# A third branch's up units for tokens 128 to 255 moved behind the first expert query, on a one-core hybrid decoder layer

## The chip, the core and the metric

One core of one Trainium2 chip runs the whole layer in one launch. The metric is the device time of an execution in microseconds (us), lower is better. Engines are named as the profile names them: PE is TensorE, with PEld its weight loads, DVE is VectorE, ACT is ScalarE, POOL is GpSimd, SP is SyncE; SPq, ACTq and POOLq are their DMA queues.

## The reference, cut to what matters

256 tokens of width 1024, all in float32. Three branches (sparse attention, RWKV-7 time mixing, cross-attention into 256 memory tokens) each give 512 values per token. They are projected up, gated and summed, projected out, and added to x. A PEER layer follows: 8 heads choose 16 of 16,384 experts per token, and each expert is one row of `u` (dotted with the token) and one row of `v` (added with the weight).

```python
up = jnp.einsum('bscw,cwd->bscd', branches, w_up.astype(F32))
gates = jax.nn.sigmoid(gate_p.reshape(B, S, N_BRANCH, D).astype(F32) + gate_bias.astype(F32))
merged = jnp.sum(gates * up, axis=2).astype(h.dtype)
h = h + merged @ w_out
h = h + peer_ffn(rmsnorm(h, ffn_norm_gain), peer_w_q, peer_key1, peer_key2, peer_u, peer_v)
...
# in peer_ffn: q = xn @ w_q; scores against two key tables; top 16 of each side; top 16 of the 256 sums
hid = jax.nn.gelu(jnp.einsum('td,ted->te', xt.astype(F32), ue), approximate=False)
return jnp.einsum('te,ted->td', gt * hid, ve).astype(xt.dtype)
```

## The kernel before

**Two tiles of tokens.** Tile 0 is tokens 0 to 127, tile 1 is tokens 128 to 255. Nearly all of on-chip memory is one tensor, `pool_mem`, cut by hand into parts that are used again as their earlier contents are done.

**The first part.** Projections, attention, memory attention and RWKV run in an order written out by hand, `SCHEDULE`. Weights come as blocks of 1 MB (`BLOCK`, 2048 columns) through a ring of three (`wring`), which SP refills when the projection unit that used a block is done (`proj_full`). Products go to two PSUM banks in turns (`begin_unit`, `begin_bank`, `unit_read`).

**The up units.** There are 12, four to a branch, two to a weight block. Branch order is memory, attention, RWKV. Units 8 to 11 (RWKV) need `y_rwkv`, which comes from `ytok` after the group norm, by PE transposes (job `("yt", t)`) and an ACT copy. DVE multiplies each unit with its gate and adds it into `merged` (function `up`, L1863 and L1865). Tile 1's norm is `("norm", 1)`, its transposes are `("out", 1)`, and both stand ahead of unit 8.

**From there to the first gather.** Four output blocks for tile 0 (`out_block`, L1085) give `h_tok`; DVE adds x (L1885). The first query (head 0, tile 0: `query_part(0, ...)`, L1101) goes from PE to ACT (L1420), PE computes the key scores (L544), ACT copies them (L1483), DVE chooses (`first_eight`, then `choose(0, FIRST)`), and POOL issues the first gather (L2143). What DVE waits for ahead of the x add is `late_in`: x, the gain row and the keys, three DMAs that ACT issues after its copy of tile 1's `y_rwkv`.

**The gathers.** There are 256: 2 tiles, 8 heads, 16 choices. One gather brings one expert of each of 128 tokens, 8 KB a token, 1.05 MB in all, to one of 8 slots. Gather number s waits for `group_free` of s + 1. In this kernel POOL gives 3 at the start, since only slots 0 to 2 hold nothing then; slots 3 to 6 hold the four output weight blocks (`out_w`) until tile 1's output blocks have used them, and the eighth holds x (`x_again`) until tile 1's sum is made; these give 4 and 1 more. After that each group that PE adds gives one. A gather of group g + 8 thus waits for PE's addition of group g.

**One group** (`dots`, `gelu`, `add_group`): DVE dots 128 rows with the token (L2042), ACT does Gelu, weight and a diagonal (L1458, L1462, L1465), PE adds the weighted rows to the sum with 8 matmul rows of 512 columns (L1126), and POOL may issue the next gather.

**The order behind the first query on PE:** key scores 0, tile 1's four output blocks, `begin_sums(0)`, first half of the second query (head 1), group 0, second half, group 1, key scores 1, the transposes of tile 1 (`ht1`, L1166), groups 2 and 3, then the queries of heads 2 to 7 for both tiles with groups between them as `QUERY_GROUPS` says (groups before, between the halves, after). ACT's order: groups 0 and 1, copy of query 1, group 2, copy of scores 1, group 3, `h_root(1)`, the eight `ht1` copies (L1494), group 4 and on. ACT holds one table of functions at a time, so Gelu, Sqrt and Exp in turns cost a table load.

**Query weights.** SP loads the eight 1 MB blocks of `peer_q` to places that become free: blocks 0, 1, 2 and 7 to the ring, 3 to 6 to `spare` parts. Block 7 waits for `("rest", 0)`, the third query.

Of the kernel before, what the change touches and what calls it, by code (L numbers as in the profile page):

```python
# [13 lines left out]
P = 128  # L14
D = 1024
# [23 lines left out]
SLOTS = 8  # L39
GROUP = 1  # L40
# [5 lines left out]
QUERY_GROUPS = [None, None, (4, 2, 4)] + [(10, 4, 2)] * 6 + [(8, 4, 4)]  # L46
EARLY = 4
# [9 lines left out]
SEEN = [(0, 0), (1, 0), (1, 1)]  # L57
N_GATE0 = 2
# [3 lines left out]
         ("gate0", N_GATE0), ("q", 2), ("k", 2), ("gate", N_GATE), ("up", 12), ("out", 4), ("first", 2), ("ht1", 2), ("rest", 8)]  # L62
# [16 lines left out]
for _name, _n in [("ident", 128), ("pick_pairs", 32), ("rot", 128), ("causal", 128),  # L79
                  ("gram_mask", 4 * CHUNK), ("level", CHUNK * LEVELS), ("iota", 16), ("inv_freq", 1), ("two_idents", CHUNK), ("to_heads", W)]:  # L80
    CONST[_name] = (_c, _n)
    _c += _n
CONST_COLS = _c

# [10 lines left out]
def constants():  # L95
# [19 lines left out]
    out["iota"] = np.tile(np.arange(16), (P, 1))  # L115
# [5 lines left out]
    out["inv_freq"] = col[:, None]  # L121
# [92 lines left out]
def build(nc, t_in, out):  # L214
    ctx = ExitStack()
    with ctx:
# [6 lines left out]

        const = sb("const", [P, CONST_COLS])
        vec = sb("vec", [P, VEC_COLS])
        trig = sb("trig", [P, 2, S])
        lora = sb("lora", [P, W])
        glora = sb("glora", [P, W])
        rows = sb("rows", [P, 2 * W])
        small = sb("small", [P, 272])  # L230
        ones = sb("ones", [P, P])
        pos_i = sb("pos_i", [P, S], I32)
        pool_mem = sb("pool_mem", [P, POOL_COLS])
# [101 lines left out]
        x_again = part(Q0 + 72 * K1, TILES, D)  # L335
# [6 lines left out]
        out_w = [part(RING0 + BLOCK * (3 + i), KT, 256) for i in range(4)]  # L342
# [52 lines left out]
        def sm(i, n=1):  # L395
# [45 lines left out]
            "ps_full", "ps_free", "stage_ok", "stage_used", "choose", "experts_ok", "gate_in", "gsum", "gate_ok",  # L441
# [5 lines left out]
        spare_in = [sem(f"spare_in{i}") for i in range(len(spare))]  # L447
        out_in = [sem(f"out_in{i}") for i in range(4)]
        slot_in = [sem(f"slot_in{i}") for i in range(SLOTS)]

        def query_weights(i):


            if 3 <= i < 7:
                return spare[i - 3], spare_in[i - 3], 16
            b = FIRST_BLOCK["out"] + (i if i < 3 else 5)
            return wring[b % RING], weights_in[b % RING], 16 * (b // RING + 1)
# [100 lines left out]
        def query_unit(e):  # L558
            return ("first", e) if e < 2 else ("rest", e - 2)
# [8 lines left out]
        def _(sp):  # L568
# [38 lines left out]
            load_query(5, proj_full, FIRST_UNIT["up"])  # L607
# [21 lines left out]
        def _(pe):  # L629
# [420 lines left out]
            def up(half=None):  # L1050
# [8 lines left out]
                for tokens_ in (slice(0, S),) if u != 8 else (slice(0, P), slice(P, S)):  # L1059
                    if u == 8:  # L1060
                        wait_read(pe, ("yt", tokens_.start // P))
                    for m in range(2) if half is None else (half,):
                        for k in range(4):
                            ins = mm(o[:, m, tokens_], lhsT=w[:, 4 * (u % 2) + k, m * P:(m + 1) * P], rhs=ys[u // 4][:, k, tokens_],  # L1064
                                     start=(k == 0), stop=(k == 3))
# [13 lines left out]
            def out_block(o, i, t):  # L1079

                pe.wait_ge(out_in[i], 16)
                for k in range(KT):
                    if t == 0 and i == 0 and k % 2 == 0:
                        pe.wait_ge(sg["merged_ok"], k // 2 + 1)
                    ins = mm(o, lhsT=merged[:, k, t * P:(t + 1) * P], rhs=out_w[i][:, k, :],  # L1085
# [76 lines left out]
            key_scores(pe, mm, 1)  # L1162
            for u in range(2):
# [4 lines left out]
            add_groups(2)  # L1168
# [25 lines left out]
        def _(act):  # L1194
# [184 lines left out]
            def chunk_out(t):  # L1379
# [11 lines left out]
            def gate(half=None):  # L1391
                if half != 0:
# [6 lines left out]
                      "exp": attention_exp}  # L1399
# [10 lines left out]
            def h_root(t):  # L1410
                act.wait_ge(sg["h_ssq"], t + 1)
# [37 lines left out]
            def gelu(par, n, g, t, k):  # L1449
# [16 lines left out]
                if g == (6 if t == 0 and k == 0 else 3):  # L1466
# [741 lines left out]
```

## Time and profile before

| what | value |
|---|---|
| median of three executions | 1043.28 us (1042.62 to 1045.35) |
| the profiled execution, its own time | 1044.32 us |
| its span in the trace | 1042.5 us |
| PE, DVE, ACT, POOL busy | 80%, 62%, 38%, 33% |
| the first gather is issued | 393.51 us |
| the last gather is issued | 1020.07 us |
| bytes moved in all | 329.67 MB, 268.45 MB of them by gathers |

The page is one execution. Its times run from the start of the span. A row of the chain of waits names what the end of the program hung on at that time. A row of windows gives busy time of each engine, then the granted clock of TensorE as a share of 2.4 GHz, then the DMA engines' busy share and what they moved.

### The profile page before, as it was taken

What the parts mean: (1) busy time and instruction counts of PE and PEld (TensorE: products, weight loads), DVE (VectorE), ACT (ScalarE), POOL (GpSimd) and SP (SyncE); (2) the same over time, 40 slices, a digit from 0 to 9 for tenths busy, and PEclk for the clock granted to TensorE, in tenths of its full rate; (3) what the DMA queues carried; (4) which work ended last, traced back from release to release, by engine and by line L of the source; (5) the groups of instructions that cost most, each with busy time, mean ns of one, the idle gap of its engine ahead of it and who ended that gap; (6) DMA issues with size and microseconds to landing.
All of it is one profiled execution on the core that took longest, in us unless ns stands there. A gap on an engine that the chain in (4) does not pass through costs nothing.

```text
span 1042.5 us, 16585 instructions
## 1 busy us (share of the span) xinstructions
PE 830.9 (80%) x5840; PEld 484.2 (46%) x5840; DVE 642.4 (62%) x1564; ACT 394.4 (38%) x1124; POOL 343.1 (33%) x313
## 2 busy tenths in 40 slices
PE   9999999999999999876776776766666666666665
PEld 8887888878888886432332332321111111111111
DVE  4543550387343538786686686686686786786784
ACT  2026152215321113544544544534443443443443
POOL 2000000611021004444444444554445445445441
PEclk9999999999999999878978977878657757757756
DMA  9443423222223588999999999999999999999996
GB/s 349 142 154 124 159 96 131 98 82 83 83 88 117 188 362 334 398 427 426 426 427 427 426 427 427 427 426 425 426 426 427 428 428 426 428 428 428 428 427 274
DMA packets 46875, 329.67 MB, mean 316 GB/s; under 512 B 5344, under 2 KB 5600, under 8 KB 7520
## 3 DMA queue, kind: packets, MB, share of 16 engines
q0 software_dynamic: 36864, 268.45, 61.2%
q1 hardware_dynamic: 9104, 57.65, 15.5%
q10 hardware_dynamic: 848, 2.75, 0.7%
q8 instruction: 41, 0.67, 0.2%
q14 instruction: 18, 0.15, 0.0%
HBM read 327.78 MB, written 1.05 MB: 315 GB/s over the span
## 4 chain that ended last, share of the span: by engine, by line
PE 50%; DMA 27%; DVE 13%; issue 5%; ACT 4%; POOL 0%; POOLq 0%; DVEq 0%; ACTq 0%; SPq 0%
DMA pool_mem<-in_experts,pool_mem 27%; PE psum_proj L659 11%; PE psum_job L1126 7%; PE psum_proj L1038 7%; DVE pool_mem L2042 5%; PE psum_proj L1101 5%; PE psum_proj L1064 4%; PE psum_proj L672 3%; PE psum_job L902 2%; DVE pool_mem L1932 1%; PE psum_job L1085 1%; PE psum_proj L1085 1%; ACT pool_mem L1465 1%; DVE pool_mem L1929 1%; ACT pool_mem L1462 1%
## 5 line engine op out<-in xcount | busy, mean ns | idle before, releaser
L1126 PE MATMUL psum_job<-pool_mem 64*64 64x512 f32 x2048 | 356.1, 808 | 199.1 <-ACT pool_mem L1465 199.0
L2143 POOL DMA_INDIRECT pool_mem<-in_experts,pool_mem x256 | 303.9, 1187 | 392.0 <-PE psum_job L1126 269.7
L2042 DVE CUSTOM_DVE_ANT_0 pool_mem<-pool_mem 128x1024 f32<-128x1024 f32 x256 | 309.8, 1224 | 165.0 <-DMA pool_mem<-in_experts,pool_mem 163.9
L1126 PEld LDWEIGHTS psum_job<-pool_mem 64*64 64x64 f32 x2048 | 83.5, 162 | 448.6 <-issue 447.6
L1458 ACT ACTIVATE pool_mem<-pool_mem 128x1 f32<-128x1 f32 x256 | 51.5, 201 | 261.7 <-DVE pool_mem L2042 261.2
L659 PE MATMUL psum_proj<-pool_mem 128*128 128x256 f32 x544 | 118.9, 379 | 0.0
L659 PEld LDWEIGHTS psum_proj<-pool_mem 128*128 128x128 f32 x544 | 103.0, 190 | 15.1 <-issue 1.3
L1465 ACT ACTIVATE pool_mem<-const,pool_mem 128x64 f32<-128x64 f32 x256 | 89.1, 348 | 18.4
L1462 ACT ACTIVATE pool_mem<-pool_mem 128x1 f32<-128x1 f32 x256 | 75.4, 295 | 9.3
L1038 PE MATMUL psum_proj<-pool_mem 128*128 128x256 f32 x320 | 74.0, 384 | 0.0
L1101 PE MATMUL psum_proj<-pool_mem 128*128 128x256 f32 (+1 forms) x320 | 67.6, 369 | 4.8 <-ACT pool_mem L1494 2.5
L1101 PEld LDWEIGHTS psum_proj<-pool_mem 128*128 128x128 f32 x320 | 55.8, 211 | 30.0 <-issue 24.6
L1038 PEld LDWEIGHTS psum_proj<-pool_mem 128*128 128x128 f32 x320 | 59.2, 190 | 10.2 <-issue 2.4
L2104 POOL TENSOR_TENSOR pool_mem<-pool_mem,small 64x256 f32<-64x256 f32 x8 | 4.9, 608 | 171.7 <-PE psum_job L835 171.2
L2123 POOL TENSOR_TENSOR pool_mem<-pool_mem,const 128x256 f32<-128x256 f32 x24 | 16.9, 726 | 98.1 <-PE psum_job L902 54.8
L1064 PE MATMUL psum_proj<-pool_mem 128*128 128x256 f32 (+1 forms) x208 | 45.3, 370 | 0.0
L1064 PEld LDWEIGHTS psum_proj<-pool_mem 128*128 128x128 f32 x208 | 35.9, 190 | 4.9 <-issue 0.2
L1527 DVE RECIPROCAL pool_mem<-pool_mem 128x256 f32<-128x256 f32 x5 | 8.6, 1739 | 43.5 <-ACT pool_mem L1217 41.5
L1281 ACT ACTIVATE pool_mem<-psum_proj,vec 128x256 f32<-128x256 f32 x24 | 10.1, 471 | 60.7 <-PE psum_proj L1038 58.7
L672 PE MATMUL psum_proj<-pool_mem 128*128 128x256 f32 x128 | 28.0, 379 | 0.0
L672 PEld LDWEIGHTS psum_proj<-pool_mem 128*128 128x128 f32 x128 | 24.3, 190 | 3.4
L1805 DVE TENSOR_TENSOR pool_mem<-pool_mem,psum_job 128x256 f32<-128x256 f32 x34 | 12.9, 418 | 17.6 <-PE psum_job L902 16.8
(296 smaller groups left out, 845.8 us busy)
## 6 DMA issues: line engine op xcount, KB each, us to landing
pool_mem<-in_weights SPq DMA_DIRECT2D x50, 1024.0 KB, 5.0
pool_mem<-in_experts,pool_mem POOLq DMA_INDIRECT x256, 12.9
pool_mem<-in_weights ACTq DMA_DIRECT2D x2, 512.0 KB, 6.4
pool_mem<-in_xT SPq DMA_DIRECT2D x2, 512.0 KB, 6.3
pool_mem<-in_memT SPq DMA_DIRECT2D x1, 1024.0 KB, 10.8
pool_mem<-in_x ACTq DMA_DIRECT2D x1, 1024.0 KB, 13.2
const<-in_const SPq DMA_DIRECT2D x1, 824.5 KB, 14.3
rows<-in_rows SPq DMA_DIRECT2D x1, 512.0 KB, 16.1
```

The costliest lines, as they stand in the source:

```text
L659: ins = mm(o[:, m, :], lhsT=w[:, k, m * P:(m + 1) * P], rhs=src[:, k, :], start=(k == 0), stop=(k == KT - 1))
L672: ins = mm(o[:, t, :], lhsT=src[:, k, t * P:(t + 1) * P], rhs=w[:, k, :], start=(k == 0), stop=(k == KT - 1))
L902: return mm(o[strip, CHUNK * i:CHUNK * i + CHUNK], lhsT=left[blocks[b], h, :], rhs=c("two_idents")[blocks[b]] if right is None else right[ ...
L1038: ins = mm(o[:, m, :], lhsT=w[:, k, m * P:(m + 1) * P], rhs=nT[:, k, :], start=(k == 0), stop=(k == KT - 1))
L1064: ins = mm(o[:, m, tokens_], lhsT=w[:, 4 * (u % 2) + k, m * P:(m + 1) * P], rhs=ys[u // 4][:, k, tokens_], start=(k == 0), stop=(k == 3))
L1101: ins = mm(o[:, m, columns(tiles)], lhsT=w[:, k, m * P:(m + 1) * P], rhs=hT[:, k, columns(tiles)], start=(m == ms[0] and k == 0 or len(ms) ...
L1126: ins = mm(sum_bank(t, d)[sum_strip(i, d), :], lhsT=diag[rows_, g % DIAGS, :], rhs=slot[g % SLOTS][rows_, D + 512 * d:D + 512 * d + 512], ...
L1458: A(act_h[:, par, col], hid[:, par, col], ACT.Gelu).then_inc(sg["gelu_ok"], 1)
L1462: A(weight[:, par, col], act_h[:, par, col], ACT.Copy, scale=gate_e[:, par, col]).then_inc(sg["weighed"], 1)
L1465: A(diag[:, g % DIAGS, :], c("two_idents"), ACT.Copy, scale=weight[:, par, col]).then_inc(sg["diag_ok"], 1)
L2042: ins = V.tensor_tensor_reduce(u, u, xn_tok[:, t, :], 1.0, 0.0, ALU.mult, ALU.add, hid[:, par, s_:s_ + 1])
L2143: G_.indirect_dma_start(slot[s_ % SLOTS], None, t_in["experts"], bass.IndirectOffsetOnAxis(ap=expert_i[:, par, s_:s_ + 1], axis=0)).then_i ...
```

## The change

1. **Units 8 to 11 compute tile 0 only.** Job `("out", 1)` leaves `SCHEDULE`. The transposes of `ytok` for tile 1 are put between the first query and its key scores; ACT copies them to `y_rwkv` after the copy of that query.
2. **Two new units, `late` 0 and 1,** follow key scores 0 on PE. Each takes one of the last two up blocks, which stay in the ring, for 128 tokens and all four quarters of 128 columns. DVE merges them (`late_merges`, four-quarter operations of 512 columns) between `first_eight` and `choose(0, FIRST)`. Tile 1's output blocks wait for these merges.
3. **Places.** The small tensors are allocated so that `params` (lora, glora, rows) and the later part of `tables` (constants, angles, positions) can hold query blocks 1 and 2. The output blocks lie in slots 4 to 7 instead of 3 to 6. x is loaded straight into `h_tok`, so `x_again` is gone. POOL starts with 4 free slots.
4. **When they are loaded.** x, the gain row and the keys are issued by ACT at a new step `("load",)` behind up unit 3; output blocks 0 to 2 after job `("Y", 3)`; block 3 after the norm; query 0 and the others after up unit 7. Query block 7 waits for `late` 0.
5. **The order behind it.** PE: group 0, half of query 1, group 1, half, group 2, key scores 1, group 3, transposes, groups 4 to 7 (`EARLY` 8), then query 2 with 0, 2, 2 groups. ACT squares tile 1's `h_tok` in `h_root(1)` (DVE did). DVE's side steps of the first 16 groups stand after groups 2, 7, 8, 10 and 11.

```diff
-QUERY_GROUPS = [None, None, (4, 2, 4)] + [(10, 4, 2)] * 6 + [(8, 4, 4)]
-EARLY = 4
+QUERY_GROUPS = [None, None, (8, 2, 2)] + [(10, 4, 2)] * 6 + [(8, 4, 4)]
+EARLY = 8
+SOFTENED = 4
...
-    ("rhs", 2), ("up", 0), ("u", 2), ("up", 1), ("y", 2), ("up", 0), ("rhs", 3), ("up", 1), ("u", 3), ("y", 3),
-    ("norm", 1), ("up",), ("up",), ("out", 1),
+    ("rhs", 2), ("up", 0), ("u", 2), ("up", 1), ("load",), ("y", 2), ("up", 0), ("rhs", 3), ("up", 1), ("u", 3), ("y", 3),
+    ("norm", 1), ("up",), ("up",),
...
-            load_query(0, proj_full, FIRST_UNIT["up"] + 8)
-            load_query(3, proj_full, FIRST_UNIT["up"] + 8)
-            sp.wait_ge(sg["y_ready"], TILES)
-            for i in range(4):
-                sp.dma_start(out_w[i] ...)
-            load_query(4, sg["y_ready"], TILES)
-            load_query(1, proj_full, FIRST_UNIT["up"] + 10)
-            load_query(2, proj_full, FIRST_UNIT["up"] + 12)
+            load_query(1, sg["gn_scale_ok"], TILES)
+            wait_job(sp, ("Y", NCHUNK - 1))
+            for i in range(3):
+                load_out(i)
+            load_query(0, proj_full, FIRST_UNIT["up"] + 8)
+            sp.wait_ge(sg["y_ready"], TILES)
+            load_out(3)
+            load_query(2, proj_full, FIRST_UNIT["up"] + 8)
+            load_query(3, proj_full, FIRST_UNIT["up"] + 8)
+            load_query(4, proj_full, FIRST_UNIT["up"] + 8)
             load_query(6, sg["merged_ok"], 4)
-            load_query(7, proj_full, FIRST_UNIT["rest"] + 1)
+            load_query(7, proj_full, FIRST_UNIT["late"] + 1)
...
+            pe.wait_ge(sg["y_ready"], TILES)
+            for i in range(CT):
+                ins = tr(psum_job[:, 1, i * P:i * P + P], ytok[:, 1, i * P:i * P + P], ident)
+            ins.then_inc(sg["y1_full"], 1)
             pe.wait_ge(late_in, 48)
             key_scores(pe, mm, 0)
+            pe.wait_ge(sg["y1_ok"], 1)
+            for j in range(LATE):
+                o = begin_bank(unit("late", j))
+                b = FIRST_BLOCK["up"] + 4 + j
+                for q in range(2):
+                    for m in range(2):
+                        for k in range(4):
+                            ins = mm(o[:, q, m * P:m * P + P], lhsT=wring[b % RING][:, 4 * q + k, m * P:(m + 1) * P],
+                                     rhs=y_rwkv[:, k, P:S], start=(k == 0), stop=(k == 3))
+                ins.then_inc(proj_full, 1)
...
             begin_sums(0)
-            o = begin_bank(unit("first", 1))
+            add_groups(1)
+            o = begin_bank(unit("second", 0))
             query_part(1, o, range(KT), (0,))
-            pe.wait_ge(sg["h1_ok"], 2)
-            pe.sem_inc(sg["group_free"], 1)
             add_groups(1)
             query_part(1, o, range(KT), (1,)).then_inc(proj_full, 1)
             add_groups(1)
             key_scores(pe, mm, 1)
+            add_groups(1)
+            pe.wait_ge(sg["h1_ok"], 2)
             for u in range(2):
...
-            add_groups(2)
+            add_groups(EARLY - 4)
...
+                    act.wait_ge(sg["h1_ok"], 2)
+                    A(xn_tok[:, 1, :], h_tok[:, 1, :], ACT.Square, accum_out=sm(HS + 1)).then_inc(sg["h_ssq"], 1)
...
+            def late_merges():
+                for j in range(LATE):
+                    wait_unit(dve, "late", j)
+                    gt = gates[:, 16 + 4 * j:20 + 4 * j, P:S]
+                    m4 = merged[:, 4 * j:4 * j + 4, P:S]
+                    unit_read(V.tensor_tensor(gt, ubank("late", j).rearrange("p (a b) -> p a b", a=4), gt, ALU.mult), "late", j)
+                    wait_unit_read(dve, "late", j)
+                    V.tensor_tensor(m4, m4, gt, ALU.add).then_inc(sg["merged_ok"], 1)
...
             first_eight()
+            late_merges()
             choose(0, FIRST)
...
-            pool.sem_inc(sg["group_free"], 3)
+            pool.sem_inc(sg["group_free"], FREE_SLOTS)
```

## Rows read from the trace of the kernel before

**Rows 1.** The page: the row of the gathers in its list of groups.

```profile
L2143 POOL DMA_INDIRECT pool_mem<-in_experts,pool_mem x256 | 303.9, 1187 | 392.0 <-PE psum_job L1126 269.7
```

**Rows 2.** Windows: busy time of each engine, clock, DMA share, GB/s.

```profile
core 0: us, PE busy (x) PEld busy (x) DVE busy (x) ACT busy (x) POOL busy (x), PEclk, DMA share, GB/s
393.50:400.00 6.50, 6.50 (x32) 5.72 (x31) 5.94 (x33) 0.00 (x0) 3.83 (x4) 1.00 0.71 222
400.00:426.00 26.00, 23.31 (x143) 15.44 (x142) 23.80 (x73) 15.08 (x41) 10.22 (x10) 0.93 1.01 425
426.00:434.00 8.00, 7.43 (x53) 4.20 (x51) 7.96 (x15) 4.50 (x13) 4.86 (x4) 1.00 0.94 338
434.00:1030.00 596.00, 397.71 (x2224) 127.76 (x2224) 424.68 (x1069) 260.88 (x826) 284.97 (x241) 0.76 1.01 427
```

**Rows 3.** Chain of waits, 349 to 406 us: start, us, what.

```profile
349.61 7.11 PE psum_proj L1064 x32
356.71 0.44 PE psum_job L679 x4
...
357.16 14.17 PE psum_proj L1064 x80
...
386.92 2.69 PE psum_proj L1101 x24
...
390.83 13.83 PE psum_job L1085 x64
...
404.80 1.09 PE psum_job L1136 x8
```

**Rows 4.** Timeline of DVE: start, us, operation, idle before.

```profile
356.37 0.69 DVE L1863 TENSOR_TENSOR pool_mem<-psum_proj,pool_mem 128x512 f32<-128x512 f32 x1
...
377.25 0.42 DVE L1885 TENSOR_TENSOR pool_mem<-psum_proj,pool_mem 128x256 f32<-128x256 f32 x1 [4.39 <-DMA pool_mem<-in_keysT]
...
396.24 0.17 DVE L1970 CAST pool_mem<-pool_mem 128x7 uint32<-128x7 f32 x1
...
404.99 1.22 DVE L2042 CUSTOM_DVE_ANT_0 pool_mem<-pool_mem 128x1024 f32<-128x1024 f32 x1
```

**Rows 5.** The line that loads the four output blocks: issue to landing.

```profile
DMA to landing us min/median/max: 12.6/17.2/20.3
```

**Rows 6.** Timeline: the first gather, gather 12, query block 7.

```profile
393.51 1.11 POOL L2143 DMA_INDIRECT pool_mem<-in_experts,pool_mem  x1 [68.33 <-DVE pool_mem L1943]
...
425.08 0.94 POOL L2143 DMA_INDIRECT pool_mem<-in_experts,pool_mem  x1 [7.56 <-PE psum_job L1126]
...
428.78 0.33 SPq L588 DMA_DIRECT2D pool_mem<-in_weights  x1
```

**Rows 7.** Timeline of ACT, 410 to 419 us.

```profile
410.91 0.37 ACT L1420 COPY pool_mem<-psum_proj 128x256 f32<-128x256 f32 x1 [1.40 <-PE psum_proj L1101]
...
412.57 0.47 ACT L1483 ACTIVATE pool_mem<-psum_job,small 128x256 f32<-128x256 f32 x1 [0.48 <-PE psum_job L544]
413.16 0.20 ACT L1458 ACTIVATE pool_mem<-pool_mem 128x1 f32<-128x1 f32 x1
...
414.09 1.28 ACT L1412 ACT_TABLE_LOAD   x1
...
415.58 2.16 ACT L1494 ACTIVATE pool_mem<-psum_proj,vec 128x128 f32<-128x128 f32 x8
417.76 1.28 ACT L1458 ACT_TABLE_LOAD   x1
```

**Rows 8.** Timeline of ACT: a square of 1024 columns, without table load.

```profile
75.12 1.04 ACT L1237 ACTIVATE pool_mem<-pool_mem 128x1024 f32<-128x1024 f32 x1
```

**Rows 9.** PE's third query and two groups in timeline; a window.

```profile
417.84 5.38 PE L1101 MATMUL psum_proj<-pool_mem 128*128 128x256 f32 x16 [2.54 <-ACT pool_mem L1494]
...
451.95 3.69 PE L1126 MATMUL psum_job<-pool_mem 64*64 64x512 f32 x16 [2.86 <-ACT pool_mem L1465]
...
419.40:422.40 3.00, 3.00 (x9) 2.37 (x8) 2.83 (x10) 1.27 (x5) 0.00 (x0) 0.50 1.01 429
```

More of the change, by code:

```diff
@@ L39 @@
 SLOTS = 8
+FREE_SLOTS = 4
 GROUP = 1
@@ L57 @@
 SEEN = [(0, 0), (1, 0), (1, 1)]
+LATE = 2
 N_GATE0 = 2
@@ L61 @@
 UNITS = [("rwkv", 7), ("mem_k", 2), ("mem_v", 2), ("mem_q", 2), ("idx_q", 1), ("idx_k", 1), ("v", 2),
-         ("gate0", N_GATE0), ("q", 2), ("k", 2), ("gate", N_GATE), ("up", 12), ("out", 4), ("first", 2), ("ht1", 2), ("rest", 8)]
+         ("gate0", N_GATE0), ("q", 2), ("k", 2), ("gate", N_GATE), ("up", 12), ("out", 4), ("first", 1), ("late", LATE), ("second", 1), ("ht1", 2), ("rest", 8)]
 STREAM = [("rwkv", 7), ("mem_k", 2), ("mem_v", 2), ("mem_q", 2), ("idx_q", 1), ("idx_k", 1), ("v", 2),
@@ L83 @@
 CONST_COLS = _c
+KEPT_COLS = CONST["rot"][0]
 VEC = {}
@@ L114, in constants @@
         [(s // (2 << l) == t // (2 << l)) & ((t >> l) % 2 == 1) & ((s >> l) % 2 == 0) for l in range(LEVELS)], axis=1)
-    out["iota"] = np.tile(np.arange(16), (P, 1))
+    out["iota"] = np.tile(np.arange(64) % 16, (P, 1))
     inv = (np.float32(1.0) / (np.float32(500000.0) ** (np.arange(0, 16, 2, dtype=np.float32) / np.float32(16))))
@@ L120, in constants @@
             col[q] = inv[(q % HD) % 8]
-    out["inv_freq"] = col[:, None]
+    out["inv_freq"] = np.stack([col, col], axis=1)
     return np.ascontiguousarray(np.concatenate([out[n] for n in CONST], axis=1).astype(np.float32))
@@ L221, in sem @@
             return ctx.enter_context(nc.semaphore(name))
[L224 to L229, printed above, removed]
+        pool_mem = sb("pool_mem", [P, POOL_COLS])
+        params = sb("params", [P, 4 * W])
+        tables = sb("tables", [P, CONST_COLS + 3 * S])
         small = sb("small", [P, 272])
         ones = sb("ones", [P, P])
-        pos_i = sb("pos_i", [P, S], I32)
-        pool_mem = sb("pool_mem", [P, POOL_COLS])
+        vec = sb("vec", [P, VEC_COLS])
+        lora, glora, rows = params[:, 0:W], params[:, W:2 * W], params[:, 2 * W:4 * W]
+        const = tables[:, 0:CONST_COLS]
+        trig = tables[:, CONST_COLS:CONST_COLS + 2 * S].rearrange("p (a b) -> p a b", a=2)
+        pos_i = tables[:, CONST_COLS + 2 * S:CONST_COLS + 3 * S].bitcast(I32)
         def part(at, *shape):
@@ L341, in build @@
         spare = [part(Y0, KT, 256), part(Q0, KT, 256), part(N0, KT, 256), part(T0 + 16 * K1, KT, 256)]
-        out_w = [part(RING0 + BLOCK * (3 + i), KT, 256) for i in range(4)]
+        out_w = [part(RING0 + BLOCK * (FREE_SLOTS + i), KT, 256) for i in range(4)]
+        over_params = params.rearrange("p (a b) -> p a b", a=KT)
+        over_tables = tables[:, KEPT_COLS:KEPT_COLS + BLOCK].rearrange("p (a b) -> p a b", a=KT)
         slot = [part(RING0 + BLOCK * i, BLOCK) for i in range(SLOTS)]
@@ L558, in query_unit @@
         def query_unit(e):
-            return ("first", e) if e < 2 else ("rest", e - 2)
+            return (("first", 0), ("second", 0))[e] if e < 2 else ("rest", e - 2)
         def columns(tiles):
@@ L1058, in up @@
                 o, w = open_unit("up", u, u // 2, half)
[L1059 to L1065, printed above, removed]
+                if u == 8:
+                    wait_read(pe, ("yt", 0))
+                tokens_ = slice(0, S if u < 8 else P)
+                for m in range(2) if half is None else (half,):
+                    for k in range(4):
+                        ins = mm(o[:, m, tokens_], lhsT=w[:, 4 * (u % 2) + k, m * P:(m + 1) * P], rhs=ys[u // 4][:, k, tokens_],
+                                 start=(k == 0), stop=(k == 3))
                 if half != 0:
@@ L1084, in out_block @@
                         pe.wait_ge(sg["merged_ok"], k // 2 + 1)
+                    if t == 1 and i == 0 and k % 4 == 0:
+                        pe.wait_ge(sg["merged_ok"], 4 + k // 4 + 1)
                     ins = mm(o, lhsT=merged[:, k, t * P:(t + 1) * P], rhs=out_w[i][:, k, :],
@@ L1398, in _ @@
                       "y": chunk_y_copy,
-                      "exp": attention_exp}
+                      "exp": attention_exp, "load": load_late}
             for step in SCHEDULE:
@@ L1478, in _ @@
                 copy_query(e)
+                if e == 0:
+                    act.wait_ge(sg["y1_full"], 1)
+                    nc.scalar.copy(y_rwkv[:, :, P:S], psum_job[:, 1, :].rearrange("p (a b) -> p a b", a=CT)).then_inc(sg["y1_ok"], 1)
                 if e == 1:
@@ L1852, in up @@
                 br, grp = u // 4, u % 4
-                gt = gates[:, 2 * u:2 * u + 2, :]
-                m2 = merged[:, 2 * grp:2 * grp + 2, :]
+                tokens_ = slice(0, S if br < 2 else P)
+                gt = gates[:, 2 * u:2 * u + 2, tokens_]
+                m2 = merged[:, 2 * grp:2 * grp + 2, tokens_]
+                tmp, new = tmp_up[:, :, tokens_], halves(ubank("up", u))[:, :, tokens_]
                 if grp == 0:
@@ L1859, in up @@
                 if br == 0:
[L1860 removed]
+                    unit_read(V.tensor_tensor(m2, new, gt, ALU.mult), "up", u)
                     wait_unit_read(dve, "up", u)
                 else:
[L1863 removed]
+                    unit_read(V.tensor_tensor(tmp, new, gt, ALU.mult), "up", u)
                     wait_unit_read(dve, "up", u)
[L1865 removed]
+                    ins = V.tensor_tensor(m2, m2, tmp, ALU.add)
                     if br == 2:
```

58 lines of the change are left out of this document (30 added, 28 removed).

## The prediction

> **What bounds the kernel now.** I read the page first. The gathers' row has 256 of them, and POOL's idle time before them is put down mostly to PE's additions, which hand back the slots [rows 1]. A wait for a slot is harmless while the other slots' transfers keep the memory path full, so I cut the span into windows by what DMA does [rows 2]. From 434 to 1030 us it moves 427 GB/s without a dip, for 596 us. A gather of 1.05 MB then takes 2.46 us, and no compute engine is near its limit (PE 398 of 596 us). So in that stretch the end hangs on bytes alone, and the only questions are when gathering starts and how full the path is until it is full for good. The windows answer the second: 222 GB/s from 393.5 to 400, 425 to 426 us, and 338 from 426 to 434. That is 1.44 + 11.05 + 2.70 = 15.2 MB by 434 us. The dip at 426 follows gather 12, which is issued at 425.08 after 7.56 us without an issue [rows 6], when 12.5 MB, twelve gathers' bytes, are nearly through. Last I read the chain of waits ahead of the first gather: from 349.61 us it is PE without a gap, 7.11 us for units 6 and 7, 0.44 for tile 1's transposes, 14.17 for units 8 to 11, then output blocks and query [rows 3].
>
> My measure for the change is therefore: how many bytes are through at 434 us, plus how many are still to come.
>
> **What the change does ahead of the first gather.** Units 8 to 11 are 80 rows in 14.17 us. A row of 256 columns costs 7.11 / 32 = 0.222 us, one of 128 columns 2.69 / 24 = 0.112 [rows 3]. The four units for tile 0 alone are 64 rows of 128 columns: 7.1 us. That saves 7.0 to 7.1. The 0.44 us of transposes goes too, but unit 8 needs the bank of unit 6, which DVE reads at 356.37 for 0.69 us because the norm holds it until then [rows 4]: unit 8 can start at 357.1, as before. So the transposes' removal is worth about 0.05. They come back for 0.44 us behind the query, where PE stands still for ACT's copy of it, 0.37 us [rows 7]: from the query's end at 389.61 to the output blocks at 390.83 are 1.22 us [rows 3], the key scores among them. ACT's extra copy of 512 columns (twice the columns of the 0.37 us) goes on while PE makes the scores. Both cost nothing on this path, and about 0.5 each if that cover is gone.
>
> A shorter PE path needs its data sooner. Before, DVE waits 4.39 us for the keys until 377.25 [rows 4], which PE's queued blocks hide, and the output blocks land 12.6 to 20.3 us after issue [rows 5]: output block 0 at about 370.2, to be used at 371.3. With these loads where they were, 7 us less of PE would have met late data. The change moves x, gain and keys to about 339 us, where DMA is idle, and the first three output blocks to about 350. In SP's queue at 2.46 us a block, the fourth lands at about 368 to 371 and is needed at 375; query 0 at about 366, needed at 378.5. So no wait is left, and **the first gather is issued at 393.51 - 7.1 = 386.4 us**. Past that queue, query block 7 is issued at about 387.5, when the DMA engines have one gather, instead of 428.78 in the full stretch [rows 6]: 1.05 MB, 2.46 us, leaves the part that sets the end.
>
> **What it adds behind the first gather.** Late 0 and 1 are 64 rows of 128 columns, 7.1 us, behind key scores 0. The saving of 7.1 us is used up there: tile 1's output blocks run from 390.9 to 404.8, where they ran before from 390.83 [rows 3]. DVE's four merge operations of 0.69 us (as in rows 4) end at about 390.9 and 392.6; the second is needed by the fifth of eight contractions, at 392.7. `choose(0, FIRST)`, which ran from 396.4 to the first dot at 404.99 [rows 4], starts at 392.6, so that the first dot is at about 401.2. Slots 4 to 7 come free with the output blocks at about 395, 398.5, 402 and 405.3, one earlier than before in number, since x holds none. The late units thus do not starve DMA by themselves: eight gathers and block 7 are 9.4 MB, and start by 390.
>
> Everything that frees a ninth to thirteenth slot, however, begins at 404.8 as before, while the bytes run 7 us and one block ahead. By the new order:
> - PE: sums to 405.9, group 0 to 407.0, half query to 409.0, group 1 to 410.0, half query to 412.0.
> - ACT copies that query (0.37) and only then does group 2, 0.9 us (from 413.16 to 414.07 is one group, rows 7): diagonal at 413.2. PE adds group 2 to 414.3, key scores to 415.0. ACT copies the scores (0.47) and does group 3, to 416.5; PE adds it to 417.6. Before, PE had scores 1 at 412.5 and ACT ended group 3 at 414.07 [rows 7]. PE and ACT wait for each other twice, 2.5 us in sum.
> - ACT then squares 1024 columns: 1.04 us [rows 8], and about 0.2 more for its sum (my estimate, from the smallest ACT rows shown). Sqrt's table and Sqrt take 1.49 (414.09 to 415.58), the eight copies 2.18, Gelu's table 1.28 [rows 7], group 4 0.9: with the short gaps between them diagonal 4 is ready at about 423.9.
> - PE adds group 4 until 424.9. Before, group 4 followed the half query that ended at 423.22 [rows 9], took 1.0, and gather 12 came 0.9 later. So gather 12 is issued at **425.9 us**, 426.7 if the matmuls run at half clock.
>
> The square in rows 8 follows a Sigmoid without a load. Whether it needs one behind Gelu no row shows; the bounds are 0 and 1.28, and I take 0, as in the nearest row. The Trainium skill (ScalarE activation tables: per-element evaluation and per-set limits, section "What a function is on this engine") says that functions in different sets are one load apart and those in one set need none; the loads of the trace, 1.28 us, agree, and by the dearer case gather 12 would be at 427.2.
>
> Gather 12 is issued as late as before (425.08), although gathers 0 to 11 and block 7, 13.6 MB, are through by about 423.5. The path stands idle until about 2 us after the issue (the first gather's bytes also took about 2).
>
> **Sum.** At 427.9 us there are 13.6 MB through, and 6.1 us more at 427 GB/s less about 0.2 MB for the ramp give 16.0 at 434, against 15.2: 0.8 MB or 2.0 us ahead. Block 7 is in both sums. The half-clock case: PE is idle from 417.6 to about 423.8. Before, an idle time of 2.5 us ahead of 417.84 was followed by a granted clock of 0.50, which is 1.2 GHz, from 419.4 to 422.4, and the half query took 5.38 us, where 16 rows of 256 columns are 3.55 at 0.222; at 0.5 two groups take 3.69, 1.85 each [rows 9], where the same 8 rows take 1.09 for the sums [rows 3]. The new idle time is longer. Then gather 12 is at 426.7, the lead at 434 is 1.2 us, and gathers 16 to 18 (behind half queries of 3.6 to 5.4 us) may be up to 1 us late again. The page TensorE: Matmul & The Clock Gate of the Trainium skill (Part 1) puts it as a default of half clock that activity lifts; the trace agrees, and by it the change pays more than before. Between 2.0 and about 0.8 I take 1.5 us. The profiled execution took 1044.32 us with a span of 1042.5, so it would take 1042.8; the median of the runs is 1.0 below its own time, so the forecast is 1043.28 - 1.5 = **1041.8 us**.
>
> **Rivals.** (1) *The whole lead survives.* Had slots come in time, the end would move by 7.1 for the start and 2.46 for block 7, about 9: 1034. For it speaks that the queue in rows 2 stayed full to 426 with the same hand-backs; against it, that gathers 9 to 12 would have to be issued 7 us earlier and PE reaches tile 1's sums at the same 404.8. 8%. (2) *Part of it.* Gather 12 comes at or below 424.5, because the two mutual waits or the copies cost less than I add up, or the dip before cost more: 3.2 to 6 us, 1037 to 1040. 24%. (3) *Slower: the ACT chain with its extra square, the extra table and a half clock makes gathers 12 to 18 late.* From gather 12 at about 431.5 the end is over 3.1 us later: 1047. That takes 5 us more than my sum, the table gives 1.3, the clock 0.8 to 2. 8%. (4) *The first gather is not earlier*, because a block or x is late: the bytes then have no lead, block 7 still moves; 1041 to 1044. 5%. My forecast, 1040.2 to 1044.5: 55%.
>
> A measurement of this kernel tells about 0.3%, 3.1 us, from no change. Faster by more: cases 1 and 2, 0.32. Slower: 0.08. Within: 0.60. The range from 1037 to 1044.8 leaves out case 1, a little of 2, and case 3. Its core, 1040.2 to 1043.5, is the forecast's own.
>
> **What the profile after would show.** Right: first gather at 386.4; block 7 at about 387.5; chain of waits with L1064 near 7 us; tile 1's output blocks end near 404.8; ACT's table load for Sqrt at about 417.8; POOL idle before gather 12, DMA below half around 424 to 427.5; a clock of 0.5 within 422 to 429. Wrong: a full DMA row from 395 us on (case 1), or output blocks that start after 392 (the merges are late), which moves all of it.

## The result, and the profile after

The changed kernel takes **1053.01 us** (median of four executions, 1052.07 to 1053.18), the kernel before 1043.80 (four, 1042.62 to 1045.35). The ratio is 1.0087, interval 1.0073 to 1.0101. That is slower by 9 us, where 1041.8 was forecast, and outside the range. The profiled execution took 1053.16 us with a span of 1051.3. Two executions far above all others of their kernels, one of e6 at 2558 us and one of the kernel before at 4113 us, are left out of the ratios and of e6's median.

**Ahead of the first gather nearly all came as predicted.** The chain of waits of the changed kernel (start, us, what), which answers to [rows 3]:

```profile
349.75 7.10 PE psum_proj L1077 x32
...
357.31 7.38 PE psum_proj L1077 x64
...
382.96 0.44 PE psum_job L1162 x4
...
384.19 7.29 PE psum_proj L1173 x64
391.48 13.96 PE psum_job L1100 x64
...
405.57 1.09 PE psum_job L1151 x8
```

Units 8 to 11 take 7.38 us instead of 14.17. The late units stand behind the query with 7.29, so that tile 1's output blocks start at 391.48 (390.9 predicted) and its sums at 405.57. POOL's and SP's timelines (start, us, instruction, idle time before it), beside [rows 6]:

```profile
386.88 1.11 POOL L2192 DMA_INDIRECT pool_mem<-in_experts,pool_mem  x1 [61.55 <-DVE pool_mem L1992]
...
427.02 1.98 POOL L2192 DMA_INDIRECT pool_mem<-in_experts,pool_mem  x1 [6.88 <-PE psum_job L1141]
...
1028.97 0.94 POOL L2192 DMA_INDIRECT pool_mem<-in_experts,pool_mem  x1 [0.31 <-issue]
...
387.94 0.33 SPq L596 DMA_DIRECT2D pool_mem<-in_weights  x1
```

The first gather is at 386.88 (386.4 predicted), 6.6 us earlier than before, query block 7 at 387.94 (387.5). Gather 12 is at 427.02 (425.9, or 426.7 at half clock). But the last gather, which stood at 1020.07, stands at 1028.97. The windows by the predicted stages, which answer to [rows 2], tell where that comes from (the last two columns are the DMA engines' busy share and GB/s):

```profile
386.50:393.00 6.50, 6.50 (x53) 6.24 (x52) 5.75 (x24) 0.00 (x0) 3.46 (x4) 1.00 0.67 242
393.00:400.00 7.00, 7.00 (x34) 6.20 (x33) 6.53 (x27) 1.68 (x3) 2.26 (x3) 1.00 1.01 426
400.00:422.00 22.00, 16.19 (x110) 10.80 (x108) 17.42 (x49) 8.95 (x27) 8.51 (x7) 1.00 0.97 375
422.00:430.00 8.00, 5.80 (x28) 1.99 (x32) 7.35 (x21) 7.06 (x20) 2.68 (x2) 0.59 0.33 118
424.00:430.00 6.00, 5.80 (x28) 1.99 (x32) 5.52 (x14) 5.13 (x17) 2.68 (x2) 0.50 0.14 29
430.00:434.00 4.00, 4.00 (x23) 2.89 (x16) 2.91 (x5) 3.26 (x10) 2.68 (x3) 0.97 0.90 350
434.00:1030.00 596.00, 393.28 (x2235) 130.35 (x2233) 420.09 (x1061) 258.03 (x813) 276.74 (x240) 0.77 1.01 421
```

Two things are to be read here.

*Up to 434 us* the stages hold 1.57 + 2.98 + 8.25 + 0.94 + 1.40 = 15.15 MB (each GB/s by its width, without the inner row 424 to 430). Before it was 15.2, and 16.0 were predicted. The prediction had most of the lead of 7.1 us and a block gone by 434; measured, all of it is gone (the start came 6.6 us earlier).

*From 434 on* the DMA engines are as busy as before (1.01), and no engine is near its limit (PE 393 of 596 us), but they move **421 GB/s instead of 427**. The 427 x 596 = 254.5 MB then take 604.5 us: 8.5 more. The profiled executions differ by 1053.16 - 1044.32 = 8.8 us, so this is nearly the whole result.

The DMA queue of the gathers from 500 to 900 us (packets, MB, and the share of 16 engines' time that the packets took), first before, then after:

```profile
q0 software_dynamic: 23327, 169.90, 100.6%
```

```profile
q0 software_dynamic: 23019, 167.63, 100.8%
```

Packets and bytes fell by 1.3% at a full share: a packet takes on average 16 x 400 us x 1.006 / 23327 = 0.276 us before and 0.280 after. So it is not a wait between transfers; the transfers themselves are slower. Between issue and landing nothing else of the stretch changed, except where the rows go to. The allocation of on-chip memory differs: the change puts `pool_mem`, which holds the slots, ahead of all other tensors instead of behind them. Each slot lies a multiple of 512 bytes behind the start of `pool_mem`, so its start modulo 256 (the remainder when divided by 256) is that of `pool_mem`. From the allocation of the two programs:

```
kernel            pool_mem starts at byte    modulo 256
before            36352 = 142 x 256          0
after             16512 = 64 x 256 + 128     128
```

### The profile page after: what moved, and what is told of

It is laid out like the page before. It is cut to its first block, busy times and chain, and to the rows that moved or that the text cites. A ratio compares the mean times of both kernels' runs of the same rounds, so it can differ in the third digit from the quotient of the medians.

```text
span 1051.3 us, 16684 instructions
## 1 busy us (share of the span) xinstructions
PE 827.2 (79%) x5888; PEld 485.1 (46%) x5888; DVE 642.6 (61%) x1566; ACT 395.3 (38%) x1126; POOL 336.1 (32%) x313
## 3 DMA queue, kind: packets, MB, share of 16 engines
HBM read 327.81 MB, written 1.05 MB: 313 GB/s over the span
## 4 chain that ended last, share of the span: by engine, by line
PE 49%; DMA 26%; DVE 12%; ACT 7%; issue 5%; POOL 1%; DVEq 0%; POOLq 0%; ACTq 0%; SPq 0%
DMA pool_mem<-in_experts,pool_mem 25%; PE psum_proj L672 11%; PE psum_job L1141 9%; PE psum_proj L1051 7%; DVE pool_mem L2091 5%; PE psum_proj L1077 4%; PE psum_proj L1116 3%; PE psum_proj L685 3%; PE psum_job L915 2%; DVE pool_mem L1981 1%; ACT L1494 1%; PE psum_job L1100 1%; PE psum_proj L1100 1%; ACT L1482 1%; ACT pool_mem L1501 1%
## 5 line engine op out<-in xcount | busy, mean ns | idle before, releaser
L2192 POOL DMA_INDIRECT pool_mem<-in_experts,pool_mem x256 | 296.3, 1158 | 408.2 <-PE psum_job L1141 291.2
L672 PEld LDWEIGHTS psum_proj<-pool_mem 128*128 128x128 f32 x544 | 103.0, 190 | 15.1 <-issue 1.3
L1501 ACT ACTIVATE pool_mem<-tables,pool_mem 128x64 f32<-128x64 f32 x256 | 89.0, 348 | 18.4
L1051 PEld LDWEIGHTS psum_proj<-pool_mem 128*128 128x128 f32 x320 | 59.2, 190 | 10.2 <-issue 2.4
L2172 POOL TENSOR_TENSOR pool_mem<-pool_mem,tables 128x256 f32<-128x256 f32 x24 | 17.0, 728 | 97.6 <-PE psum_job L915 54.1
L1116 PE MATMUL psum_proj<-pool_mem 128*128 128x256 f32 (+1 forms) x224 | 47.6, 368 | 0.0
L1116 PEld LDWEIGHTS psum_proj<-pool_mem 128*128 128x128 f32 x224 | 39.0, 200 | 18.5 <-issue 14.5
L1077 PE MATMUL psum_proj<-pool_mem 128*128 128x256 f32 (+1 forms) x192 | 38.5, 352 | 0.5 <-issue 0.5
L1077 PEld LDWEIGHTS psum_proj<-pool_mem 128*128 128x128 f32 x192 | 30.5, 190 | 4.3 <-issue 0.8
L1456 ACT COPY pool_mem<-psum_proj 128x512 f32<-128x512 f32 (+1 forms) x10 | 5.0, 500 | 55.6 <-PE psum_proj L1116 55.6
L685 PEld LDWEIGHTS psum_proj<-pool_mem 128*128 128x128 f32 x128 | 24.3, 190 | 3.4
```

The costliest lines, as they stand in the source:

```text
L672: ins = mm(o[:, m, :], lhsT=w[:, k, m * P:(m + 1) * P], rhs=src[:, k, :], start=(k == 0), stop=(k == KT - 1))
L685: ins = mm(o[:, t, :], lhsT=src[:, k, t * P:(t + 1) * P], rhs=w[:, k, :], start=(k == 0), stop=(k == KT - 1))
L1051: ins = mm(o[:, m, :], lhsT=w[:, k, m * P:(m + 1) * P], rhs=nT[:, k, :], start=(k == 0), stop=(k == KT - 1))
L1116: ins = mm(o[:, m, columns(tiles)], lhsT=w[:, k, m * P:(m + 1) * P], rhs=hT[:, k, columns(tiles)], start=(m == ms[0] and k == 0 or len(ms) ...
L1501: A(diag[:, g % DIAGS, :], c("two_idents"), ACT.Copy, scale=weight[:, par, col]).then_inc(sg["diag_ok"], 1)
L2192: G_.indirect_dma_start(slot[s_ % SLOTS], None, t_in["experts"], bass.IndirectOffsetOnAxis(ap=expert_i[:, par, s_:s_ + 1], axis=0)).then_i ...
```

## The experiments

Theory A: the start address of the slots sets the rate. Rival B: the change's traffic does (query block 7 early, other places of weights). Rival C: where the gathered rows lie in DRAM, which the inputs' sizes set. Underneath A a second question was left: why an earlier start and an early block 7 brought nothing.

### The address alone, in both kernels

**e1**, the kernel before with one unused tensor ahead of `pool_mem`, which is the last tensor of that kernel, so that nothing else moves:

```diff
         pos_i = sb("pos_i", [P, S], I32)
+        sb("pad", [P, 32])
         pool_mem = sb("pool_mem", [P, POOL_COLS])
```

> The kernel before with one unused tensor of 32 columns (128 bytes a partition) allocated ahead of pool_mem, so that the slots start at byte 36480 of a partition instead of 36352, 128 bytes past a multiple of 256, as in the changed kernel. Nothing else differs. Theory A, the start address of the slots sets how fast gathers are written: the full stretch from 434 us on falls from 427 to 421 GB/s, 254 MB then take 8.5 us more, about 1052. Theory B, what costs is on the DRAM side (the constants grew by 49 columns and the arrays behind them lie elsewhere) or in the order of the instructions: 427 GB/s and 1043.5 as before.

Measured: 1052.07 us, ratio 1.0086 (1.0066 to 1.0107). The full stretch in its windows:

```profile
434.00:1030.00 596.00, 393.61 (x2200) 127.16 (x2200) 420.69 (x1062) 258.26 (x818) 283.26 (x241) 0.75 1.01 421
```

**e7**, the same with 16 columns, 64 bytes (`sb("pad", [P, 16])`).

> The kernel before with 16 unused columns ahead of pool_mem, so that the slots start 64 bytes past a multiple of 256 (36416). If a start off the 256-byte grid costs whatever its distance, because each row of 8 KB then touches 33 pieces of 256 bytes instead of 32: 421 GB/s in the full stretch and 1052, as with 128. If the grain is 64 bytes, or the loss grows with the distance: 427 GB/s and 1044.5, or about half the loss, 1048.

Measured: 1053.31 us, ratio 1.0084 (1.0059 to 1.0109), so a smaller distance does not cost less.

```profile
460.00:1030.00 570.00, 378.64 (x2106) 120.88 (x2104) 400.74 (x1005) 245.72 (x778) 267.97 (x228) 0.75 1.01 421
```

**e2** and **e3**, the changed kernel with 96 columns (the diff) and 32 columns (e3) ahead of `pool_mem`, so that it starts at byte 16896 (33 x 512) and 16640 (65 x 256):

```diff
+        sb("pad", [P, 96])
         pool_mem = sb("pool_mem", [P, POOL_COLS])
```

> The changed kernel with an unused tensor of 96 columns ahead of pool_mem, so that the slots start at a multiple of 512 bytes (16896), as in the kernel before. Theory A: 427 GB/s in the full stretch, and the time is that of the kernel before within 1 us, since 15.15 MB were through at 434 us in the changed kernel and 15.2 in the one before: 1043.5. Theory B: still 421 GB/s and 1053.

> The changed kernel with 32 unused columns ahead of pool_mem: the slots start at 16640, a multiple of 256 but not of 512 bytes. Theory A with a grain of 256 bytes: as the run on 512, 427 GB/s and 1043.5. Theory A with a grain of 512: 421 GB/s, 1053. Theory B: 1053.

Measured: e2 1044.51 us, ratio 1.0007 (0.9996 to 1.0018); e3 1044.55, ratio 1.0005 (0.9993 to 1.0017), beside 1044.68 for the kernel before. The full stretch of e2, then of e3:

```profile
434.00:1030.00 596.00, 393.55 (x2261) 131.06 (x2259) 423.61 (x1067) 260.10 (x822) 275.30 (x240) 0.77 1.01 426
```

```profile
434.00:1030.00 596.00, 394.83 (x2256) 132.31 (x2252) 424.03 (x1068) 260.31 (x822) 274.31 (x240) 0.77 1.01 427
```

**e4**, the kernel before with 49 more columns in the constants' array in DRAM, which it doesn't read:

```diff
-            sp.dma_start(const[:, :], t_in["const"])
+            sp.dma_start(const[:, :], t_in["const"][:, 0:CONST_COLS])
...
-        "const": constants(),
+        "const": np.pad(constants(), ((0, 0), (0, 49))),
```

> The kernel before with the constants' array 49 columns wider in DRAM alone (the same 1649 columns are loaded), so that what lies behind it in DRAM moves as in the changed kernel, and the on-chip addresses are those of before. Theory A: 427 GB/s, 1043.5. Theory B, DRAM side: 421 GB/s, 1052.

Measured: 1044.57 us, ratio 1.0005 (0.9994 to 1.0016), 427 GB/s.

A holds. Offsets of 64 and 128 bytes cost the old kernel what the change cost, and moving the slots back to a multiple of 256 bytes takes it all from the changed one; a multiple of 512 brings nothing more. B falls with e1 (old traffic, 421) and e3 (new traffic, 427). C has nothing in e4, which tried one other layout. One thing is not separated: `pool_mem` also holds the gathers' indices and most of what the engines read, and all of it moved with the slots. The engines' work did not slow with it (DVE's dot took 1.224 us on average before and 1.226 in e1, ACT's Gelu 0.201 in both), but no run moved the slots alone. From here e3 is the base: it is the change without the address.

### Why the earlier start brings nothing

In e3 gather 12 is at 427.14, as in the changed kernel. ACT's timeline of the changed kernel from 412 us shows the chain that leads there:

```profile
412.54 0.37 ACT L1456 COPY pool_mem<-psum_proj 128x256 f32<-128x256 f32 x1 [7.86 <-PE psum_proj L1116]
...
415.63 0.47 ACT L1522 ACTIVATE pool_mem<-psum_job,small 128x256 f32<-128x256 f32 x1 [1.91 <-PE psum_job L552]
...
417.04 1.04 ACT L1446 ACTIVATE pool_mem<-pool_mem 128x1024 f32<-128x1024 f32 x1
417.99 0.19 ACT L1446 ACTIVATION_READ_ACCUMULATOR pool_mem<-pool_mem 128x1 f32 x1
418.19 1.28 ACT L1448 ACT_TABLE_LOAD   x1
419.48 0.29 ACT L1448 ACTIVATE small<-small 128x1 f32<-128x1 f32 x1
419.69 2.15 ACT L1533 ACTIVATE pool_mem<-psum_proj,vec 128x128 f32<-128x128 f32 x8
421.85 1.28 ACT L1494 ACT_TABLE_LOAD   x1
```

and PE's timeline the end of it:

```profile
417.28 1.09 PE L1141 MATMUL psum_job<-pool_mem 64*64 64x512 f32 x8 [1.68 <-ACT pool_mem L1501]
418.30 1.09 PE L1196 MATMUL psum_proj<-tables,pool_mem 128*128 128x128 f32 x8
424.20 6.62 PE L1141 MATMUL psum_job<-pool_mem 64*64 64x512 f32 x32 [4.81 <-ACT pool_mem L1501]
```

Between PE's additions of groups 1 and 4 thus stand the two mutual waits, the square, both table loads and the copies. After 4.81 us without work the granted clock is 0.50 (1.2 GHz) in the row 424 to 430 above, and four groups take 1.65 us each instead of 1.02.

**e5**, the mutual waits: ACT does group 2 before it copies the second query, and group 3 before it copies its scores.

```diff
                     soften(0, 0)
-                    gelus(2)
-            gelus(1)
+                    gelus(3)
             h_root(1)
```

> The changed kernel with slots on a multiple of 256 bytes (1044.5), and ACT does group 2 before it copies query 1, and group 3 before it copies scores 1; PE's order is kept. Theory C, the PE and ACT chain ahead of gather 12 sets what is left of the 7 us lead: both mutual waits go, gather 12 is issued about 2.4 us sooner than 427.1, and the end comes 2 to 2.4 us sooner, 1042.3. Theory D, the lead is lost to something else behind the first gather (a memory path that can't be filled so early, or slots that DVE frees late): no change, 1044.5.

Measured: 1042.57 us, ratio 0.9986 (0.9974 to 0.9997). From the first gather to gather 12 are 427.00 - 389.08 = 37.9 us, in e3 427.14 - 387.01 = 40.1. The gather's row:

```profile
427.00 1.42 POOL L2192 DMA_INDIRECT pool_mem<-in_experts,pool_mem  x1 [7.84 <-PE psum_job L1142]
```

2.2 us less on the chain, and 0.9986 / 1.0005 is 2.0 us less at the end (the two intervals overlap, from 0.9993 to 0.9997). As far as this can tell, a microsecond of the chain is one of the end here, but from times alone the gain of e5 over e3 is not shown. (In e5's profiled execution everything from about 340 us on stands 2 us later, so only distances are compared.)

**e6**, groups 4 to 7 ahead of the transposes on PE, and ahead of the square and the table loads on ACT:

```diff
             key_scores(pe, mm, 1)
-            add_groups(1)
+            add_groups(EARLY - 3)
             pe.wait_ge(sg["h1_ok"], 2)
...
-            add_groups(EARLY - 4)
...
-                    gelus(2)
-            gelus(1)
+                    gelus(3)
+            gelus(4)
             h_root(1)
```

> The changed kernel with slots on a multiple of 256 bytes, ACT does groups 2 and 3 as in the run above and then groups 4 to 7 ahead of the square, the root and the ht1 copies; PE adds groups 3 to 7 behind key scores 1 and transposes after them. Theory C: gather 12 is issued at about 417.7 instead of 427.1, the memory path has no gap before it, and the time falls by 7 to 9 us to about 1036; a late gather 16, behind a third query that now starts later, would take up to 2 us of it. Theory D: no change, 1044.5.

Measured: 1041.47 us, ratio 0.9975 (0.9964 to 0.9987); about 1036 was expected, or 1038 with a late gather 16. Gather 12 was at 417.79 as expected, and then gather 16 was late, more than the 2 us allowed for it. POOL's timeline, and the windows behind it:

```profile
417.79 0.94 POOL L2192 DMA_INDIRECT pool_mem<-in_experts,pool_mem  x1 [0.68 <-issue]
...
431.86 1.55 POOL L2192 DMA_INDIRECT pool_mem<-in_experts,pool_mem  x1 [9.41 <-PE psum_job L1142]
```

```profile
430.00:434.00 4.00, 3.99 (x26) 2.12 (x26) 4.00 (x8) 2.30 (x9) 1.83 (x2) 1.00 0.87 369
434.00:438.00 4.00, 4.00 (x28) 2.15 (x27) 2.13 (x4) 0.59 (x1) 2.07 (x2) 1.00 1.06 274
438.00:442.00 4.00, 2.04 (x19) 1.30 (x21) 1.14 (x1) 3.03 (x11) 1.51 (x2) 0.94 0.83 295
```

The gap of 424 to 430 was moved to 431 to 442, behind the third query (PE 424.83 to 429.9), which waits for the copies.

**e8** and **e12** put single parts of the change back. e8: x, gain and keys are loaded late, behind the norm, as in the kernel before.

```diff
-    ... ("up", 1), ("load",), ("y", 2), ...
-    ("norm", 1), ("up",), ("up",),
+    ... ("up", 1), ("y", 2), ...
+    ("norm", 1), ("load",), ("up",), ("up",),
```

> The changed kernel with slots on a multiple of 256 bytes, and ACT issues x, the gain row and the keys behind the second norm, about 357 us, as in the kernel before, instead of behind up unit 3; the rest is as changed. If the loads' new time carries part of the gain: they land 13 to 19 us after issue, at 370 to 376, DVE's first sum with x waits for them from about 368.5, PE stops for the bank in its third output block, and the first gather is issued 5 to 8 us later, near 393; the end comes up to 4 us later, since gather 12's chain moves too: 1048. If their time doesn't matter: 386.9 and 1044.5.

Measured: 1048.44 us (1045.59 to 1050.15), ratio 1.0029 (1.0015 to 1.0044). DVE's add of x waits for the keys, and POOL's first gather comes 6.2 us later than in e3:

```profile
375.59 0.76 DVE L1927 TENSOR_TENSOR pool_mem<-psum_proj,pool_mem 128x256 f32<-128x256 f32 x2 [8.04 <-DMA pool_mem<-in_keysT]
```

```profile
393.25 1.11 POOL L2193 DMA_INDIRECT pool_mem<-in_experts,pool_mem  x1 [66.04 <-DVE pool_mem L1993]
```

So the early loads are a needed part of the shorter path, as the prediction had it: without them the old first gather returns, 393.25 against 393.51.

e12: query block 7 waits for the third query again.

```diff
-            load_query(7, proj_full, FIRST_UNIT["late"] + 1)
+            load_query(7, proj_full, FIRST_UNIT["rest"] + 1)
```

> The changed kernel with slots on a multiple of 256 bytes, and query block 7 waits for the third query again, as in the kernel before, instead of for late unit 0. If its early load takes 1.05 MB out of the stretch that sets the end: 2.46 us slower than with the early load, 1047. If it only takes the place of gather bytes at its new time: no change, 1044.5.

Measured: 1046.97 us, ratio 1.0033 (1.0022 to 1.0044), against 1.0005 for e3: 0.28%, 2.9 us, where one block at 427 GB/s is 2.46. Block 7 is issued at 439.39.

### Versions that keep part of the lead

**e9** is e3 with both repairs: ACT does groups up to 5, then the copies, then groups 6 to 9, and only then the square, Sqrt and the second head's Exp. PE adds ten groups ahead of the third query. DVE's side steps of the second head start behind group 9.

```diff
-QUERY_GROUPS = [None, None, (8, 2, 2)] + ...
-EARLY = 8
+QUERY_GROUPS = [None, None, (10, 0, 2)] + ...
+EARLY = 10
...
                     soften(0, 0)
-                    gelus(2)
-            gelus(1)
-            h_root(1)
+                    gelus(3)
+            gelus(2)
             for u in range(2):
                 wait_unit(act, "ht1", u)
...
-            early = SOFTENED
+            gelus(EARLY - 6)
+            h_root(1)
+            soften(1, 1)
+            early = EARLY
...
-            steps = {2: (second_tile,), 7: (halves, sums, experts), 8: (h_inverse_root,), 10: (choose_gates,), 11: (h_normed,)}
+            steps = {2: (second_tile,), 9: (halves, sums, experts), 10: (h_inverse_root,), 11: (choose_gates,), 12: (h_normed,)}
```

> The changed kernel with slots on a multiple of 256 bytes and the order behind key scores 1 written anew: ACT does groups 0 to 2, copy of query 1, groups 3 to 5, the ht1 copies, groups 6 to 9, then square, root and the second softmax; PE adds groups 4 to 9 ahead of the third query, whose halves follow each other; DVE dots groups 8 and 9 ahead of choosing for head 1. Theory C: gathers 8 to 17 are issued by about 427, the two gaps (ahead of gather 12 in the changed kernel, ahead of gather 16 in the run before this) are gone, 427 GB/s from about 393 us on, and most of the 7.1 + 2.5 us lead stays: 1036 to 1037. Theory E, the memory path does not take more early bytes whatever the order, and each order only moves the gap: 1041.5 as in the run before this.

Measured: 1039.43 us, ratio 0.9955 (0.9939 to 0.9971). That lies between the two expectations, 1036 to 1037 and 1041.5: the order keeps more of the lead, but not most of it. What is late next is the first gather of the second head, which waits for DVE's choice:

```profile
431.21 1.67 POOL L2195 DMA_INDIRECT pool_mem<-in_experts,pool_mem  x1 [7.49 <-DVE pool_mem L2076]
```

**e10** is e9 without the pad, that is at byte 16512 again.

> The same order as in e9 with the slots where the changed kernel has them, 128 bytes past a multiple of 256. If the two causes are separate they add: 421 GB/s, about 8.5 us above e9, 1045. If a fuller queue hides the slower writes: less than 4 us above e9.

Measured: 1046.99 us, ratio 1.0032 (1.0019 to 1.0044), 7.6 us above e9, and 421 GB/s from 460 to 1020 us against 427. 8.5 us was expected if the two causes add, under 4 if the fuller queue hid one: they add.

**e11** spreads the choice over groups 7, 8 and 9:

```diff
-            steps = {..., 9: (halves, sums, experts), ...}
+            steps = {..., 7: (halves,), 8: (sums,), 9: (experts,), ...}
```

> As e9, but DVE chooses for head 1 in three pieces, behind groups 7, 8 and 9, where in e9 it stood still for landings of gathers 6 to 9 (1.2 to 2.4 us before each) and then chose in one piece, which released gather 16 only at 431.2. Gather 16 should be issued at about 427; the windows of 389, 344 and 387 GB/s from 430 to 442 us are worth 1.5 us at most. Theory C: 0.5 to 1.5 us below e9, 1038.5. Theory E: as e9, 1039.4.

Measured: 1038.34 us, ratio 0.9960 (0.9944 to 0.9976). The same gather of POOL, and the whole stretch in one window (353 GB/s in the changed kernel, 384 in e9; 364 in the kernel before, with 0.7 MB of weights up to 393.5 in it):

```profile
426.80 1.67 POOL L2195 DMA_INDIRECT pool_mem<-in_experts,pool_mem  x1 [2.51 <-DVE pool_mem L2076]
```

```profile
386.00:460.00 74.00, 61.00 (x392) 37.93 (x392) 63.98 (x189) 34.98 (x105) 35.28 (x30) 0.93 0.96 395
```

Gather 16 is 4.4 us earlier than in e9, but the two intervals overlap: that e11 beats e9 is not shown, though its median is the lowest of all kernels here. Both beat the kernel before by 0.4% and the changed one by 1.3%.

How many bytes the gathers' queue has moved by 460 us tells what each order is worth. All these runs have their slots on a multiple of 256 bytes; from 460 to 1020 us all move 427 GB/s, and the same 1.05 MB of weights are still to come:

| run | gathers' MB, 380 to 460 us | ahead of the kernel before, at 427 GB/s | profiled execution, against 1044.32 us |
|---|---|---|---|
| before | 25.15 | | |
| e8 | 22.46 | -6.3 us | 5.8 us slower |
| e12 | 24.16 | -2.3 us | 2.4 us slower |
| e3 | 24.94 | -0.5 us | 0.8 us slower |
| e6 | 26.60 | 3.4 us | 2.5 us faster |
| e9 | 27.31 | 5.1 us | 4.9 us faster |
| e11 | 28.11 | 6.9 us | 6.7 us faster |

So within a microsecond the end follows the bytes that are through, and e3's earlier start had been spent by then.

## Why the prediction was wrong, point by point

- **The failed step: "From 434 to 1030 us it moves 427 GB/s", read from the kernel before and carried over to the changed kernel.** The prediction counted bytes and divided by this rate, and gave none of the change's "Places" a price, although that part of the diff moves the tensor into which 268 of 330 MB are written. Measured: 421 GB/s, 8.5 us. e1 and e7 show the loss in the old kernel from the address alone, e2 and e3 take it from the new one. No rival had it: the slower one was a late ACT chain. Its price could not be read from the trace of before, where all slots start on one address modulo 256; but that the base moves by 19840 bytes, 77.5 times 256, follows nearly from the sizes of the tensors that stood ahead of it (19804 bytes), and a term of unknown size for it would have belonged into the range.
- **Start of the gathers:** right. 386.88 against 386.4, so 6.6 us earlier for the 7.1 in the sum; units 8 to 11 took 7.38 against 7.1, behind a step of 0.46; no wait for x, keys or blocks. The early loads carry it (e8).
- **Block 7:** right. 387.94 against 387.5. 2.46 us were predicted, and e12 puts it at 2.9.
- **Late units and merges:** right. 7.29 us for 7.1; the merges run from 389.81 to 392.93, the first dot at 401.36 for 401.2.
- **No table load for the square behind Gelu:** right, the 1.04 us row at 417.04 follows group 3's rows on ACT (its Gelu is at 416.22) without a load. The one load of Sqrt, 1.28 us, stands behind it.
- **The lead at 434 us:** mis-sized, the second failed term. Predicted were 0.8 MB or 2.0 us (0.8 to 2.0, taken 1.5), measured was none: 15.15 for 15.2 MB. Even without the address the forecast of 1.5 us less, a ratio of 0.9986, does not come: e3 has 1.0005, from 0.9993 up. Gather 12 came 1.1 us after the main case, 0.47 MB. The ramp, the stretch in which the path fills again, was the rest: for the 7 us from its issue to 434 the path moves 0.17 + 1.40 = 1.57 MB, where the sum's rule gives 5.0 us at 427 less 0.2 MB, 1.9, for that issue.
- **Half clock:** right. 0.50 in 424 to 430, four groups at 1.65 us; gather 12 at 427.02 fits this case's 426.7.
- **Rival 2** ("because the two mutual waits or the copies cost less than I add up"): the waits cost 2.2 us (e5) for the 2.5 stated, the eight copies 2.15 for 2.18. The sum for gather 12 held; e9 and e11 show what it takes to get that rival's time, another order on two engines and DVE.

What stays open: why a start off 256 bytes costs 1.4%. An 8 KB row touches 33 pieces of 256 bytes instead of 32 when it starts between two of them, 3.1% more pieces; the packets took 1.5% longer, and equal cost at 64 and at 128 bytes fits. This is argued, not shown. The Trainium skill (DMA: Bandwidth & Descriptors, section "How a descriptor splits into AXI transactions") says that a transaction must start on a 256-byte address, so that a transfer which starts elsewhere has a first transaction from the boundary below, with bytes that are fetched and not used. It tells this of reads, and no trace here shows transactions; in these runs the loss came and went with the place written to (e1, e3), which the page does not speak of. Open too is how to keep the rest of the lead, 6.6 us and a block of 2.46: e9 and e11 keep 4 to 5 of these 9.1 us by their ratios, 6.7 in e11's profiled execution, the fastest of its six.

## What to carry to other kernels

When a diff touches the order or the size of allocations, work out the start of every buffer that large transfers write to, and keep it on a multiple of 256 bytes; a pad of 32 columns was worth 8.5 us of 1053. When a stretch hangs on bytes alone, its GB/s is a term of the sum and needs a reason why it should stay. And a head start in front of a fixed chain (here ACT's between groups 1 and 4) turns into a gap unless the chain moves too; the first reordering only moves the gap (e6), so look at once for what is late next.

## What the runs showed of the hardware that was not expected

Gathers of 8 KB rows into on-chip memory ran at 427 GB/s with destinations on a multiple of 256 bytes (bases 36352 and 16640; 426 at 16896) and at 421 with bases 64 or 128 bytes past one (36416, 36480, 16512), with the DMA engines' busy share at 1.01 in both: the share does not show the loss, only GB/s and time per packet (0.276 and 0.280 us) do.
